# Hybrid decoder step: attention probabilities scaled by the reciprocal of their sum on GpSimd before the transposes, in place of a spread of the denominators by matmul

## The reference

```python
def attend(q, kg, vg, valid):
    logits = jnp.einsum('bqhd,bqkhd->bqhk', q.astype(jnp.float32), kg.astype(jnp.float32)) * (HEAD_DIM ** -0.5)
    logits = jnp.where(valid[:, :, None, :], logits, NEG_INF)
    p = jax.nn.softmax(logits, axis=-1)
    out = jnp.einsum('bqhk,bqkhd->bqhd', p, vg.astype(jnp.float32))
```

## Time and profile before

| | us |
|---|---|
| median of 3 runs (1465.22 to 1471.34) | 1466.41 |
| the profiled execution | 1463.4 |
| its span | 1461.6 |
| TensorE matmul busy | 1365.6 (93%) |
| VectorE busy | 656.8 (45%) |
| GpSimd busy | 524.0 (36%) |
| ScalarE busy | 453.0 (31%) |
| mean granted TensorE clock | 0.983 |

### The profile page before, as it was taken

How to read it: one execution, slowest core, us unless ns; L and a number is a source line. 1 busy time by engine, 2 the same in 40 slices (tenths; PEclk the granted TensorE clock), 3 DMA queues, 4 the chain that set the end, 5 groups by cost and what they waited for, 6 DMA issues and landing times.

```text
span 1461.6 us, 25035 instructions
## 1 busy us (share of the span) xinstructions
PE 1365.6 (93%) x9477; PEld 1268.7 (87%) x9477; DVE 656.8 (45%) x1441; ACT 453.0 (31%) x985; POOL 524.0 (36%) x511
## 2 busy tenths in 40 slices
PE   1979999998879799999999999999999999999998
PEld 1855999996556699867899999999999999999998
DVE  4317998776876412215633223232232332323335
ACT  4324687745655422224321020020110201102034
POOL 5240786442431212232233343333333433333520
PEclk9889999999999999999999999999999999999999
DMA  6150112320001386586111111111111111111103
GB/s 174 38 118 15 30 52 64 119 69 1 2 1 30 111 249 215 175 247 207 44 44 44 44 44 45 45 57 44 44 44 45 44 44 47 55 44 44 58 15 120
DMA packets 129404, 107.10 MB, mean 73 GB/s; under 512 B 19736, under 2 KB 108440, under 8 KB 129279
## 3 DMA queue, kind: packets, MB, share of 16 engines
q1 hardware_dynamic: 118350, 98.49, 22.4%
q10 hardware_dynamic: 10281, 5.15, 1.3%
q0 software_dynamic: 656, 1.84, 0.6%
HBM read 94.57 MB, written 9.20 MB: 71 GB/s over the span
## 4 chain that ended last, share of the span: by engine, by line
PE 74%; DVE 7%; SPq 3%; issue 3%; ACT 2%; DMA 0%; POOL 0%; DVEq 0%; ACTq 0%
PE bank L1813 69%; PE bank L2012 2%; PE bank L1955 1%; SPq L506 1%; DVE junk L1460 1%; SPq L507 1%; DVE prob L1551 1%; ACT sjunk L997 1%; DVE cum L1519 1%; PE bank L1855 1%; DVE probT L1585 1%; DVE lack L1464 1%; DVE rstd_b L1697 0%; PE bank L2091 0%; ACT probT L916 0%
## 5 line engine op out<-in xcount | busy, mean ns | idle before, releaser
L811 POOL TENSOR_TENSOR w_hi<-w_raw,zero 128x1024 fp32r<-128x1024 f32 x60 | 113.5, 1892 | 459.8 <-PE bank L1813 443.9
L1813 PE MATMUL bank<-hn_hi,w_hi 128*128 128x384 f32 (+1 forms) x768 | 251.0, 327 | 6.1 <-DVE relu L1747 3.3
L1813 PE MATMUL bank<-hn_lo,w_hi 128*128 128x384 f32 (+1 forms) x768 | 248.7, 324 | 0.0
L1813 PE MATMUL bank<-hn_hi,w_lo 128*128 128x384 f32 (+1 forms) x768 | 247.8, 323 | 0.0
L1240 ACT ACTIVATE relu<-relu 128x384 f32<-128x384 f32 (+1 forms) x96 | 47.8, 499 | 551.0 <-DVE relu L1747 551.0
L1813 PE MATMUL bank<-hid_hi,w_hi 128*128 128x384 f32 (+1 forms) x672 | 217.7, 324 | 0.0
L1813 PE MATMUL bank<-hid_lo,w_hi 128*128 128x384 f32 (+1 forms) x672 | 217.2, 323 | 0.0
L1813 PE MATMUL bank<-hid_hi,w_lo 128*128 128x384 f32 (+1 forms) x672 | 216.3, 322 | 0.0
L1762 DVE TENSOR_TENSOR acc<-bank,acc 128x384 f32<-128x384 f32 x168 | 87.0, 523 | 207.4 <-PE bank L1813 207.4
L1813 PE MATMUL bank<-xn_hi,w_hi 128*128 128x384 f32 (+1 forms) x456 | 150.9, 331 | 1.3 <-DVE score L1401 1.3
L1813 PEld LDWEIGHTS bank<-hn_hi,w_hi 128*128 128x128 f32 x768 | 144.8, 189 | 7.9 <-issue 7.6
(11 more groups left out here) (260 smaller groups left out, 2378.7 us busy)
## 6 DMA issues: line engine op xcount, KB each, us to landing
w_raw<-in_w_ff_dram SPq DMA_DIRECT2D x64, 512.0 KB, 3.8
page<-in_cache_k_dram SPq DMA_DIRECT2D x64, 256.0 KB, 3.3
page<-in_cache_v_dram SPq DMA_DIRECT2D x64, 256.0 KB, 3.1
w_raw<-in_w_in_dram SPq DMA_DIRECT2D x18, 512.0 KB, 3.6
xrow<-in_x_prompt_dram SPq DMA_DIRECT2D x8, 512.0 KB, 7.9
w_raw<-in_w_out_dram SPq DMA_DIRECT2D x8, 512.0 KB, 4.1
xblk<-in_x_prompt_dram SPq DMA_DIRECT2D x8, 512.0 KB, 4.8
out_dram<-yrow SPq DMA_DIRECT2D x8, 512.0 KB, 2.6
```

The source lines that it names most:

```text
L811: nc.gpsimd.tensor_tensor(w_hi[n[0] % 2][:, :], w_raw[n[0] % 2][:, :], zero_w, ALU.add).then_inc(s_whi, 1)
L1813: return nc.tensor.matmul(out, lhsT, rhs, start=start, stop=stop)
```

## The change

- `share(i)` on GpSimd multiplies the probabilities of head i in prob, in place, by the reciprocal of their sum. p_T(i) waits for it (`s_shr`) and no longer for the exponential.
- `reciprocals(u)` on VectorE takes the two reciprocals of one unit, once in every unit, behind logits(u+1).
- spread, spread_T, o_share, o_norm and the tiles onorm and rdenb are gone. The values of a pair of units take 256 columns of their bank; o_high on ScalarE reads them from PSUM, and o_low, now on VectorE, too.
- `on_act`: the first halves of all heads, and all halves of the even ones, go to ScalarE.
- With two halves TensorE issues the first half of qk(u+2) between p_T(2u) and p_T(2u+1), and the second behind p_T(2u+1).
- mask_sum is cut in two, behind the shares of the first and the second unit of the next block.
- The semaphore of the values counts even units; the odd ones use that of the bank. ScalarE and SyncE wait accordingly.
- In the front, the six small loads move from ScalarE's queue to SyncE's, with semaphores of their own for g1 and for the page table; sqjunk moves away from the tile that high writes, and the batches of squares, high, scale and low alternate.

The core of the diff:

```diff
         def on_act(i, hf):
-            return hf == 0 and (n_half(heads[i][0]) == 2 or i % 2 == 0)
+            return hf == 0 or i % 2 == 0
...
+            def share(i):
+
+                j, h = heads[i]
+                pool.wait_ge(s_rd, i // 2 + 1)
+                v = prob[:, i % 4, 0:P * (j + 1)]
+                nc.gpsimd.tensor_scalar(v, v, rden[:, j % 2, h:h + 1], None, ALU.mult).then_inc(s_shr, 1)
...
+            def shares(u0, u1):
+                for u in range(u0, u1):
+                    share(2 * u)
+                    share(2 * u + 1)
+                    j = u // C4 - 1 + ranked[0] + 1
+                    if u >= C4 and j <= QB and u % C4 < 2:
+                        mask_sum(j, u % C4)
...
+            def reciprocals(u):
+
+                j, c = units[u]
+                dve.wait_ge(s_exp, 2 * u + 2)
+                nc.vector.reciprocal(rden[:, j % 2, 2 * c:2 * c + 2], den[:, j % 2, 2 * c:2 * c + 2]).then_inc(s_rd, 1)
...
+            reciprocals(0)
             for u, (j, c) in enumerate(units):
                 pT_out(2 * u)
                 pT_out(2 * u + 1)
                 if u + 2 < NU:
                     logits(u + 2)
-                if c % 2 == 1:
-                    shares(u // 2)
-                elif u >= 2:
-                    o_norm(u // 2 - 1)
+                if u + 1 < NU:
+                    reciprocals(u + 1)
+                if c % 2 == 0 and u >= 2:
+                    o_low(u // 2 - 1)
                 if j + ranked[0] + 1 <= QB:
                     if c < 3:
                         mask(j + ranked[0] + 1, c)
...
             def p_T(i):
                 j, h = heads[i]
-                pe.wait_ge(s_exp, i + 1)
+                pe.wait_ge(s_shr, i + 1)
...
             for u in range(NU):
                 p_T(2 * u)
+                early = n_half(units[u][0]) == 2 and u + 2 < NU
+                if early:
+                    qk(u + 2, (0,))
                 p_T(2 * u + 1)
-                if u + 2 < NU:
+                if early:
+                    qk(u + 2, (1,))
+                elif u + 2 < NU:
                     qk(u + 2)
-                if u % 2 == 0 and u >= 2:
-                    spread_T(u // 2 - 1)
                 pv(u)
-            spread_T(NU // 2 - 1)
...
+            sp.dma_start(g1[:, :], ln1[0].rearrange("(k p) -> p k", p=P), allow_slow_non_contiguous=True).then_inc(s_gain, 16)
             w_load(sp, 0)
+            sp.dma_start(pages[0:1, :], page_table.rearrange("b p -> (b p)").rearrange("(a n) -> a n", a=1)).then_inc(s_page, 16)
             w_load(sp, 1)
-            sp.wait_ge(s_const, 5 * 16)
+            sp.dma_start(hist[:, :], state_pool[0].rearrange("b t c -> (b t) c")).then_inc(s_hl, 16)
+            sp.dma_start(g2[:, :], ln2[0].rearrange("(k p) -> p k", p=P), allow_slow_non_contiguous=True).then_inc(s_const, 16)
...
+            sp.wait_ge(s_page, 16)
```

More of the change, by code:

```diff
@@ L470, in freeof, with wait_unit @@
             return free[plan[name][0]]
+        def wait_unit(eng, u):
+            if u % 2:
+                wait_full(eng, ("o", u // 2))
+            else:
+                eng.wait_ge(s_pvu, u // 2 + 1)
         def w_load(sp, n):
@@ L774, in mask_sum @@
-            def mask_sum(j):
-                v, r, n = rows_of(j)
-                pool.wait_ge(s_mrk, j - ranked[0])
-                nc.gpsimd.tensor_tensor(cum[0:r, 0:n], cum[0:r, 0:n], flag[0:r, 0:n], ALU.add).then_inc(s_msum, 1)
-                pool.wait_ge(s_msum, j - ranked[0])
-                nc.gpsimd.tensor_scalar(v, cum[0:r, 0:n], -NEG, NEG, ALU.mult, ALU.add).then_inc(s_mask, 1)
-            def rows_half(q0, q1):
-                for q in range(q0, q1):
-                    if q % 2 == 1 and q // 2 + ranked[0] + 1 <= QB:
-                        mask_sum(q // 2 + ranked[0] + 1)
-                    spread(q)
-                    if q >= 1:
-                        o_low(q - 1)
@@ L790, in _, with mask_sum @@
-            rows_half(0, QB + 2)
+            def share(i):
[3 more added lines that the diff above has]
+                nc.gpsimd.tensor_scalar(v, v, rden[:, j % 2, h:h + 1], None, ALU.mult).then_inc(s_shr, 1)
+            def mask_sum(j, part):
+                v, r, n = rows_of(j)
+                if part == 0:
+                    pool.wait_ge(s_mrk, j - ranked[0])
+                    nc.gpsimd.tensor_tensor(cum[0:r, 0:n], cum[0:r, 0:n], flag[0:r, 0:n], ALU.add).then_inc(s_msum, 1)
+                else:
+                    pool.wait_ge(s_msum, j - ranked[0])
+                    nc.gpsimd.tensor_scalar(v, cum[0:r, 0:n], -NEG, NEG, ALU.mult, ALU.add).then_inc(s_mask, 1)
@@ L791, in _ @@
+            def shares(u0, u1):
[5 more added lines that the diff above has]
+                        mask_sum(j, u % C4)
+            shares(0, C4 * (QB // 2) + 2)
             pool.wait_ge(s_nm, H * QB // 2)
@@ L798, in _ @@
             pool.wait_ge(s_zq, 1 + 2 * C4)
-            rows_half(QB + 2, 2 * QB)
-            o_low(2 * QB - 1)
+            shares(C4 * (QB // 2) + 2, NU)
             for n in range(N_OUT + 1, N_OUT + KM + 2):
@@ L929, in rows_out @@
                     evac(("rows", n, i), dst[0:NS, NT - 1, :], bank[b][0:NS, 0:P])
-            for i in range(3):
-                squares(i)
-            for i in range(3):
-                high(i)
+            squares(0)
+            squares(1)
+            high(0)
+            squares(2)
+            high(1)
+            high(2)
             evac("hist", ext[:, :, :, 0:HIST],
@@ L1111, in _ @@
                 if u % 2 == 0 and u >= 2:
-                    o_share(u // 2 - 1)
-                if u % 2 == 1 and u >= 3:
-                    o_high((u - 3) // 2)
-            o_share(NU // 2 - 1)
+                    o_high(u // 2 - 1)
             o_high(NU // 2 - 1)
-            act.wait_ge(s_pvu, NU)
             act.wait_ge(s_store, 2 * 16)
@@ L1344, in mean @@
                 nms[0] += 1
-            for i in range(3):
-                scale(i)
+            scale(0)
+            scale(1)
+            low(0)
+            scale(2)
+            low(1)
+            low(2)
             dve.wait_ge(s_iota, 1)
@@ L1351, in _ @@
                                         ALU.min, ALU.mult).then_inc(s_rc, 1)
-            for i in range(3):
-                low(i)
             dve.wait_ge(s_rc, C4)
@@ L1934, in _, with qk @@
                     mm(ps[:, 0:w], wpool[:, c, :], pooled[:, c, t0:t0 + w], True, True).then_inc(fullof(name), 1)
-            def qk(u):
+            def qk(u, halves=(0, 1)):
                 j, c = units[u]
-                for hf in range(n_half(j)):
+                for hf in [x for x in halves if x < n_half(j)]:
                     w = min(512, P * (j + 1) - 512 * hf)
@@ L1972, in pv @@
                                   probT[:, e, P * k:P * k + P], k == 0, k == j)
-                last.then_inc(s_pvu, 1)
-            def spread_T(q):
-                pe.wait_ge(s_rb, q + 1)
-                ps = bank[plan[("o", q)][0]]
-                for c in range(2):
-                    for e in range(2):
-                        c0 = 2 * P * c + P
-                        last = mm(ps[DH * e:DH * e + DH, c0:c0 + P], rdenb[:, q % 2, 2 * c + e, :], ident[:, :], True, True)
-                last.then_inc(fullof(("o", q)), 1)
+                last.then_inc(fullof(name) if c % 2 else s_pvu, 1)
             for c in range(C4):
```

87 lines of the change are left out of this document (29 added, 58 removed).

## The result

The changed kernel takes **1595.43 us** (median, 1594.52 to 1595.95) against 1467.22 us before: ratio 1.0869, 95% interval 1.0844 to 1.0894. The forecast of 1516 had the direction and the place right and less than half of the size: +50 forecast, +128 measured.

A forecast was written before the change was run, and what follows sets the result against it. TensorE was taken as 74% of the chain of waits, with a new ring through four engines bounding attention after the change. 1463.4 + 46 (pairs) + 4 (clock) + 0 (front) = 1513.4, median 3.0 above: 1516; range 1484 to 1550.

The forecast's parts named there:

- its 4 for the clock: Attention stage: TensorE, idle for longer, runs two or three more stretches at 1.2 instead of 2.4 GHz, some 1.5 us each: +4.
- 1. The ring: Attention: each unit's transposes wait for share, its reciprocal stands behind logits(u+2); rounds of 8.25 us in block 7 against 6.05 to 6.5.
- 1b. Share's price: GpSimd's share in the ring: 1.05 us at 1024 columns, 0.61 at 512, from the nearest TENSOR_SCALAR row.
- The rival "as much as the two-input operation": GpSimd's share costs 2.12 us instead of 1.05 at 1024 columns; the ring's shares, about 28 us, double: 1544; 10%.
- the clock's rival: Attention: the clock stays low for half of the units, +33 in place of 4, 1545; 13%.
- 2. The shared port: Blocks 0 to 5: VectorE's six mask scans hold up GpSimd's share, +2.5, +3.55, +4.4 for the first three pairs.
- The mask's third part: Blocks 0 to 5: its two-input VectorE operation can slip between two shares, +0.45 each; +0.9, +1.0, +0.8 by pair.
- 3. mask_sum: Second part stands behind the next unit's shares, VectorE's next mask part waits: +1.2 in block 5, 4.6 in five blocks.
- 4. Savings at nothing: Attention: 16 rounds of TensorE's spreading matmuls and 32 of VectorE's 48 transpose copies go, none on the ring: counted at nothing.
- the first rival: Attention: the engines' totals decide, not the ring; -3 and -11 from less spreading and fewer copies, 1452; 6%.
- 5. The front: Before attention: squares begin earlier, but TensorE waits for the gathers behind page table and 64 issues; -5 to +4, taken as 0.

## Why the prediction was wrong in size

The stretches between the first shares of blocks 0, 2, 4 and 6, and to the end of the last values (us; before as in the earlier trace rows):

| | blocks 0, 1 | 2, 3 | 4, 5 | 6, 7 | sum |
|---|---|---|---|---|---|
| before | 21.0 | 30.0 | 50.5 | 48.4 | 149.9 |
| forecast, without its 4 for the clock | 31 | 45 | 60 | 59.5 | 195 |
| share in two steps, TensorE kept busy | 31.7 | 46.8 | 64.2 | 63.5 | 206.2 |
| share in two steps | 35.6 | 55.5 | 65.4 | 67.0 | 223.5 |
| changed kernel | 40.7 | 66.3 | 81.3 | 90.7 | 279.0 |

The same ladder in medians is 1512 forecast (1516 less its 4 for the clock), 1523, 1539, 1595. With the run that has share in one step and TensorE kept busy (1568) the miss of 83 us comes apart: 11 with price and clock nearly as forecast (1523 less 1512), 45 for share's price at a clock near 1.0 (1568 less 1523), and 27 for the lower clock (1595 less 1568).

**1. The ring: right.** It closes where the forecast said, in the order that it said, and opening it (1490 with share unchanged) removes 105 of the 128 us, taking share out (1441) all of them. With share and clock nearly as forecast, the pairs miss by 0.7, 1.8, 4.2 and 4.0 us, part of it the added matmuls.

**1b. Share's price: the step that failed.** The term "share of 1024 columns: the nearest row is GpSimd's TENSOR_SCALAR, 1.05" was mis-sized. It measured 2.84, and that is worth 56 us with what it does to the clock (1595 less 1539), 45 without (above). It counted more than once: in blocks 4 to 7 the sum had one share in each round, with the other hidden behind the 1.99 of transposes and qk, and at 2.84 the other one comes out by some 0.8 us a round in block 7. The nearest row by name was a form with two arithmetic steps; share has one, and here the one-step form is the dear one. The rival "as much as the two-input operation" had the right thought, that the row might not fit, for the wrong reason: the operand from SBUF costs 0.07 us, and its upper bound of 2.12 was no bound. The range's high end of 1550 rested on it and on the clock's rival. The Trainium skill, "GPSIMD Engine Reference", section 3.1, gives 1.03 cycles an element for its shortest loops (k up to 2); at the 1.2 GHz of an example there that is an estimate of 0.86 ns, if share is such a loop. The two-step form agrees (0.84 ns a column here), the one-step form does not (2.5), and the measurement decides.

**2. The shared port: right for the scans.** In block 4 the share that starts 0.21 us after the scan takes 5.63 us for the pair in place of 3.74, 1.89 more where 1.96 was forecast. Over the six scans the pairs are longer by 0.9, 1.15, 1.4, 1.7, 1.9 and 2.0 us, 9 in all where 10.45 was forecast. The mask's third part was forecast at 2.7 in all; it lengthens the changed kernel's shares by under 0.4, but those in two steps with TensorE kept busy by 0.4 to 1.0 each, 4.5 in all, which is part of the 11 us above. Timeline of the changed kernel:

```profile
462.85 3.74 POOL L772 TENSOR_SCALAR prob<-prob,rden 128x640 f32<-128x640 f32 x2 [3.23 <-DVE rden L1579]
...
472.21 2.28 DVE L1503 TENSOR_TENSOR_SCAN cum<-eq 128x1024 f32<-128x1024 bf16 x1
472.42 5.63 POOL L772 TENSOR_SCALAR prob<-prob,rden 128x640 f32<-128x640 f32 x2 [1.34 <-DVE rden L1579]
```

**3. mask_sum: the mechanism right, the term** about 2.4 instead of 4.6 by the traces of the kernels with the cheap share. That the median came out on the forecast's term was luck: the rest of its gain lies outside the blocks with the split.

**4. Savings at nothing: right for this order** of work, since none of it was on the ring. Once share is out of the way they are some 23 to 24 us (25 less the front), where the first rival had 14 for spreading and copies.

**5. The front: right**, 1 to 2 us, inside -5 to +4, with the wait for the gathers doubled.

**6. The clock: mis-sized.** "Two or three stretches, +4" became most of the stage: about 16 us with the cheap share, 27 or more with the dear one. It had a rival of its own at +33 with 13%. That the two rivals would come together, each making the other likelier, because a dearer share leaves TensorE idle for longer, was not in the chances: they were priced one at a time, and the high end was set by one of them and not by their sum. Even the sum (1516 + 29 + 28 = 1573) would have been too low, since share cost more than its rival allowed.

What stays open is why the one-step form is slow; no run tried it on another array, out of place, or with another operation. Part of the last 11 us (the third mask part above, the added matmuls, logits at 3.42 in one round against 3.09) was not taken apart either.

## What to carry to other kernels

When a change puts an operation on the path that the trace has never shown, the nearest row must match it in the number of arithmetic steps and inputs, not only in engine and name; where none does, measure that operation by itself first, since here this one price was off by 1.8 us in each round of the widest block. Before an operation is put on a slow engine, look at what its input stands behind: against the kernel without share (1441), the same share of 2.84 us cost 154 us in the closed ring and 49 with exponentials and reciprocals one unit ahead. And a stall of TensorE can cost twice, once as the wait and once as the lower clock of the work after it, which was 27 us here.

## What the runs showed of the hardware

- On GpSimd, in-place fp32 over 128 partitions and 1024 columns: multiply alone 2.84 us with a scalar from SBUF and 2.77 with a constant; multiply and add in one instruction 1.12 with a scalar from SBUF (1.05 with constants, not in place); two inputs, one of them a broadcast column, 1.89.
- A share that started 0.1 to 0.2 us after a two-input scan on VectorE took longer by about 0.2 us less than the rest of the scan, at six widths: 0.9 to 2.0 us more beside scans of 1.2 to 2.3 us.
- Matmuls that compute nothing brought the granted clock of the stage from 0.55 to 0.79 back to 0.96 to 0.98 and made the kernel 27 us faster; 1.7 times as many (704 against 420) made it 5 us slower than the changed kernel at a clock of 1.00.
